# A heads stage, a merge and an out stage put into one block, with two staging tiles for keys and five for values

## The reference

```
h = rmsnorm(x) * (1 + sc1) + sh1
pq, pkv, pkr, hq, hf_f, hf_b, hi, hg, ga, gb = split(h @ w_in)
q  = (rmsnorm(pq) @ w_uq)                      # 8 heads, 64 + 32 columns each
kv = rmsnorm(pkv) @ w_ukv                      # keys and values of 8 heads, 64 + 64 columns each
o_mla = softmax(q k / sqrt(96)) v              # k also has 32 shared columns with a rotary position
o_hg  = gated linear recurrence (hq, hf, hi, hg)
mix = sigmoid(ga) * (o_mla @ w_mla_o) + sigmoid(gb) * (o_hg @ w_hg_o)
x = x + gt1 * (mix @ w_out)
x = x + gt2 * conv_glu(rmsnorm(x) * (1 + sc2) + sh2)
y = rmsnorm(x) * g_final
```

## Time and profile before

| | |
|---|---|
| median of 3 runs | 2144.15 us (2143.12 to 2145.16) |
| the profiled execution, its own time | 2142.61 us |
| its span, first to last instruction | 2140.8 us |
| PE busy | 2072.6 us, 97% of the span |
| mean granted clock of TensorE | 0.988 |
| DVE, ACT, POOL busy | 44%, 30%, 36% |
| transfers | 185.01 MB, mean 86 GB/s |

### The profile page before, as it was taken

How to read it: one execution, slowest core, us unless ns; L and a number is a source line. 1 busy time by engine, 2 the same in 40 slices (tenths; PEclk the granted TensorE clock), 3 DMA queues, 4 the chain that set the end, 5 groups by cost and what they waited for, 6 DMA issues and landing times. The chain is left out here.

```text
span 2140.8 us, 28026 instructions
## 1 busy us (share of the span) xinstructions
PE 2072.6 (97%) x11524; PEld 1927.2 (90%) x11524; DVE 948.8 (44%) x1386; ACT 649.6 (30%) x949; POOL 769.9 (36%) x512
## 2 busy tenths in 40 slices
PE   5999999999999989999989899999999999999998
PEld 4889999999999968888789778999999999999996
DVE  5326252525143047566545185245244333533466
ACT  4322323232223254766723211311111121112122
POOL 1143434444132234455526422432332232233290
PEclk9999999999999999999999999999999999999999
DMA  8753111112212284323375332211111111112132
GB/s 288 238 150 33 55 33 55 31 57 60 67 50 58 87 224 132 89 72 96 99 159 193 119 118 72 67 40 50 40 44 46 30 52 48 40 40 79 50 102 96
DMA packets 192961, 185.01 MB, mean 86 GB/s; under 512 B 55193, under 2 KB 159346, under 8 KB 192834
## 3 DMA queue, kind: packets, MB, share of 16 engines
q1 hardware_dynamic: 191538, 178.49, 28.3%
q0 software_dynamic: 1296, 4.72, 0.6%
HBM read 142.41 MB, written 40.78 MB: 86 GB/s over the span
## 5 line engine op out<-in xcount | busy, mean ns | idle before, releaser
L129 POOL TENSOR_TENSOR s_w_lo<-s_w_raw,s_w_hi 128x1024 fp32r<-128x1024 f32 x85 | 219.8, 2586 | 512.0 <-ACT s_w_hi L124 512.0
L2606 PE MATMUL s_ps<-h_hi,s_w_hi 128*128 128x384 f32 x1056 | 353.1, 334 | 0.7 <-ACT gate_pad L2438 0.7
L2606 PE MATMUL s_ps<-h_hi,s_w_lo 128*128 128x384 f32 x1056 | 352.9, 334 | 0.0
L2606 PE MATMUL s_ps<-h_lo,s_w_hi 128*128 128x384 f32 x1056 | 352.8, 334 | 0.0
L662 PE MATMUL s_psum<-h_hi,s_w_hi 128*128 128x384 f32 x984 | 332.9, 344 | 7.4 <-DVE h_lo L1330 7.4
L662 PE MATMUL s_psum<-h_lo,s_w_hi 128*128 128x384 f32 x984 | 325.7, 336 | 0.0
L662 PE MATMUL s_psum<-h_hi,s_w_lo 128*128 128x384 f32 x984 | 325.3, 336 | 0.0
L2606 PEld LDWEIGHTS s_ps<-h_hi,s_w_hi 128*128 128x128 f32 x1056 | 198.2, 188 | 1.5 <-issue 1.0
L662 PEld LDWEIGHTS s_psum<-h_hi,s_w_hi 128*128 128x128 f32 x984 | 185.5, 189 | 15.1 <-issue 12.1
L2606 PEld LDWEIGHTS s_ps<-h_lo,s_w_hi 128*128 128x128 f32 x1056 | 198.2, 188 | 0.4
L2606 PEld LDWEIGHTS s_ps<-h_hi,s_w_lo 128*128 128x128 f32 x1056 | 198.2, 188 | 0.0
(11 more groups left out here) (371 smaller groups left out, 3809.2 us busy)
## 6 DMA issues: line engine op xcount, KB each, us to landing
s_w_raw<-in_w_ffn_in SPq DMA_DIRECT2D x44, 512.0 KB, 3.9
s_w_raw<-in_w_in SPq DMA_DIRECT2D x41, 512.0 KB, 4.1
s_w_mod<-in_w_mod SPq DMA_DIRECT2D x8, 2048.0 KB, 8.1
w_raw<-in_w_ffn_out SPq DMA_DIRECT2D x11, 1024.0 KB
scratch_gates<-sig SPq DMA_DIRECT2D x48, 192.0 KB, 1.9
merge_gates<-scratch_gates SPq DMA_DIRECT2D x16, 576.0 KB, 4.3
scratch_o_mla<-o_raw SPq DMA_DIRECT2D x8, 576.0 KB, 5.0
scratch_x<-x SPq DMA_DIRECT2D x9, 512.0 KB, 2.6
```

The lines of the kernel that those rows point to most:

```text
L129: pool.tensor_tensor(flat[0], flat[1], flat[2], ALU.subtract).then_inc(self.lo_ready, 1)
L2606: mm = pe.matmul(ps[bank][:, 0:CH], a[s][:, k, :], b[:, k, j * CH:(j + 1) * CH], start=n == 0, stop=n == 3 * KD - 1)
```

## The change

The three stages after the projection share one block, one set of semaphores and one PSUM tensor. Each stage function now returns its five instruction lists, and every engine does its three lists one after the other, without a meeting in between. Where a later stage depends on an earlier one, it waits on that stage's semaphores. The merge's loads of weight chunks 2 and 3 are put in front of the loads that depend on the last head. The out stage's PSUM banks are numbered so that its first five are not those of the merge's last chunk. Slice 4 of w_out gets its tiles at a place that is free earlier. Its loads for slices 4 and 5 are issued at the end of the merge's list on SP.

In the expansion, key blocks alternate between two pairs of staging tiles, and the values use a ring of five pairs. The second key pair lies where the raw query weights `uq_raw` are, so block 1 waits until those have been read (`uq_lo_ready`). The two added value pairs lie where the second head's query tiles will be, so the split of that query waits for their stores.

The diff without the changes of indentation, cut to its core:

```diff
+V_RING = 5
-def stage_attention(nc, io, cst, lower, more, low, up, home):
-    with ExitStack() as ctx:
-        sems = Signals(nc, ctx, "s4")
+def stage_attention(nc, io, cst, sems, psum, lower, more, low, up, home):
+    sems.prefix = "s4"
...
-        uq_raw = b_only("uq_raw", [P, 3, HEADS * QH])
-        kst_hi, kst_lo = b_only("kst_hi", [P, NK], F32R), b_only("kst_lo", [P, NK], F32R)
+    raw_home = Arena(nc, b_only.at + 2 * NK * 4)
+    uq_raw = raw_home("uq_raw", [P, 3, HEADS * QH])
+    kst_hi, kst_lo = [b_only("kst_hi0", [P, NK], F32R)], [b_only("kst_lo0", [P, NK], F32R)]
+    kst_hi.append(b_only("kst_hi1", [P, NK], F32R))
+    kst_lo.append(b_only("kst_lo1", [P, NK], F32R))
+    spare_hi, spare_lo = Arena(nc, q_at + NT * 4), Arena(nc, q_at + 3 * NT * 4)
+    vst_hi += [spare_hi(f"vst_hi{i}", [P, 512], F32R) for i in range(3, V_RING)]
+    vst_lo += [spare_lo(f"vst_lo{i}", [P, 512], F32R) for i in range(3, V_RING)]
+    ps_s = [psum[:, 2 * i:2 * i + 2, :] for i in range(2)]
+    ps_m = [psum[:, 4 + i, :] for i in range(2)]
+    ps_o = psum[:, 6:8, :]
...
 # SP, heads stage: the stores name tile x % 2 (keys) and x % V_RING (values)
-        sp.wait_ge(k_stored, 32 * (h // 2 + 1))
+        sp.wait_ge(k_stored[h // 2 % 2], 32 * (h // 4 + 1))
-    sp.wait_ge(den_stored, 16 * (HEADS - 1))
-    for i in range(2):
-        sp.wait_ge(o_stored[i], 16 * HEADS // 2)
-    sp.wait_ge(g_loaded, 32)
...
 # ACT, a unit of the expansion (DVE waits for the same)
         if kind == "k":
-            if x > 0 and u == 0:
-                act.wait_ge(k_stored, 32 * x)
-            act.activation(kst_hi[:, a:z], ring(n)[:, 0:z - a], ACT.Copy).then_inc(u_act, 1)
+            if x == 1 and u == 0:
+                act.wait_ge(uq_lo_ready, 2)
+            if x >= 2 and u == 0:
+                act.wait_ge(k_stored[x % 2], 32 * (x // 2))
+            act.activation(kst_hi[x % 2][:, a:z], ring(n)[:, 0:z - a], ACT.Copy).then_inc(u_act, 1)
         if kind == "v":
-            if x >= 3:
-                act.wait_ge(v_stored[x % 3], 32 * (x // 3))
+            if x >= V_RING:
+                act.wait_ge(v_stored[x % V_RING], 32 * (x // V_RING))
...
 # ACT item H and POOL item G, head 1
+        if h == 1:
+            for i in range(3, V_RING):
+                act.wait_ge(v_stored[i], 32 * v_uses[i])
...
 # SP, merge: load_w(2) and load_w(3) first
+    else:
+        sp.wait_ge(att["w_lo"], c - 1)
+    load_w(2)
+    load_w(3)
+    for i in range(2):
+        sp.wait_ge(att["o_stored"][i], 16 * HEADS // 2)
+    sp.wait_ge(att["den_stored"], 16 * (HEADS - 1))
+    sp.wait_ge(att["x_lo"], KB)
     sp.dma_start(home.den9[:, :], ...)
-    load_w(2)
     load_x(KB)
     load_x(KB + 1)
-    load_w(3)
...
 # PE, merge
+    pe.wait_ge(att["x_lo"], KB)
     for c in range(CHUNKS_M):
         if c >= 2:
             pe.wait_ge(w_lo_ready, c - 1)
+        else:
+            pe.wait_ge(att["w_lo"], c + 1)
+        if c == 1:
+            pe.wait_ge(att["o_read"], 2 * HEADS)
 # DVE, merge, at the start
+    dve.wait_ge(att["gates"], 32)
     dve.wait_ge(last_loaded, 16)
...
 # out stage: banks, and tiles of slice 4
+    wo_hi, wo_lo = home.wo_hi + [first("wo_hi4", [P, D], F32R)], home.wo_lo + [first("wo_lo4", [P, D], F32R)]
+    first = Arena(nc, after_h + 2 * NT * 4)
-        ps = [ctx.enter_context(nc.psum_tensor(f"s8_ps{i}", [P, 512], F32)) for i in range(8)]
+    ps = [psum[:, i, :] for i in (0, 1, 2, 3, 7, 4, 5, 6)]
 # SP, out stage
+    sp.wait_ge(merge["quotient"], KD // 2)
     load_wo(4)
     load_wo(5)
+    sp.wait_ge(merge["bank"], 6 * KD)
+    sp.wait_ge(merge["gated"], 6 * KD)
+    sp.wait_ge(merge["m_lo"], KD)
 # ACT, out stage
-    for k in range(WO_HERE, KD):
+    act.wait_ge(merge["m_lo"], KD - 1)
+    wo_split(WO_HERE)
+    act.wait_ge(merge["gated"], 6 * KD)
+    for k in range(WO_HERE + 1, KD):
         wo_split(k)
 # POOL, out stage
+    pool.wait_ge(merge["m_lo"], KD)
 # PE, out stage
+    pe.wait_ge(merge["wo_lo"], WO_HERE)
     for k in range(KD):
         if k >= WO_HERE:
             pe.wait_ge(wo_lo_ready, k - WO_HERE + 1)
+        pe.wait_ge(merge["m_lo"], k + 1)
         for o in range(6):
+            if k == 0 and o in (0, 5):
+                pe.wait_ge(merge["gated"], 6 * KD - 3 + o // 5)
...
 # program
+    with ExitStack() as ctx:
+        sems = Signals(nc, ctx, "s4")
+        psum = ctx.enter_context(nc.psum_tensor("late_psum", [P, 8, 512], F32))
+        (att_sync, att_tensor, ...), att_links = stage_attention(...)
+        (merge_sync, merge_tensor, ...), merge_links = stage_merge(..., att_links)
+        out_sync, out_tensor, ... = stage_out_ffn(..., merge_links)
+        with nc.Block() as block:
+            @block.sync
+            def _(sp):
+                att_sync(sp)
+                merge_sync(sp)
+                out_sync(sp)
+            # tensor, scalar, vector and gpsimd alike
```

More of the change, by code:

```diff
@@ L2862, in program @@
     home = MergeHome(nc, base + half, upper, low.end)
-    stage_attention(nc, io, cst, lower, more, low, up, home)
-    assert lower.at <= upper and more.at <= HIGH
     mix = Arena(nc, base)
@@ L2868, in program, with _ @@
     partial = Arena(nc, base + half // 2)("merge_partial", [P, KD, NT])
-    stage_merge(nc, io, cst, home, m_hi, m_lo, partial)
     again = Arena(nc, base)
     h2_hi, h2_lo = again("h2_hi", [P, KD, NT], F32R), again("h2_lo", [P, KD, NT], F32R)
-    stage_out_ffn(nc, io, cst, base, m_hi, m_lo, h2_hi, h2_lo, home)
+    with ExitStack() as ctx:
+        sems = Signals(nc, ctx, "s4")
+        psum = ctx.enter_context(nc.psum_tensor("late_psum", [P, 8, 512], F32))
+        (att_sync, att_tensor, att_scalar, att_vector, att_gpsimd), att_links = stage_attention(nc, io, cst, sems, psum, lower, more, low, up, home)
+        assert lower.at <= upper and more.at <= HIGH
+        (merge_sync, merge_tensor, merge_scalar, merge_vector, merge_gpsimd), merge_links = stage_merge(nc, io, cst, sems, psum, home, m_hi, m_lo, partial, att_links)
+        out_sync, out_tensor, out_scalar, out_vector, out_gpsimd = stage_out_ffn(nc, io, cst, sems, psum, base, m_hi, m_lo, h2_hi, h2_lo, home, merge_links)
+        with nc.Block() as block:
[4 more added lines that the diff above has]
+                out_sync(sp)
+            @block.tensor
+            def _(pe):
+                att_tensor(pe)
+                merge_tensor(pe)
+                out_tensor(pe)
+            @block.scalar
+            def _(act):
+                att_scalar(act)
+                merge_scalar(act)
+                out_scalar(act)
+            @block.vector
+            def _(dve):
+                att_vector(dve)
+                merge_vector(dve)
+                out_vector(dve)
+            @block.gpsimd
+            def _(pool):
+                att_gpsimd(pool)
+                merge_gpsimd(pool)
+                out_gpsimd(pool)
 def constants():
```

2249 lines of the change are left out of this document (1121 added, 1128 removed).

## The result

The changed kernel takes **2132.39 us** (median of 5 runs, 2130.59 to 2133.57) against 2143.99 us, a ratio of 0.9948 with a 95% interval of 0.9936 to 0.9959. That is 11.6 us faster, where 21.0 had been forecast: the direction was right, the time lies 1.9 us above the range. The profiled execution took 2130.59 us, its span 2128.8 us, 12.0 less than before.

A forecast was written before the change was run, and what follows sets the result against it. PE sets the time, so only its idle time and slow clock afterwards can be won: 7.2 (expansion) + 4.7 (heads to merge) + 9.1 (merge to out) = 21.0 us, from 2144.15 to 2123.2 us, range 2118.5 to 2130.5.

The forecast's parts named there:

- The key tiles: Expansion: key block 2 no longer waits for key block 1's store; PE's 5.74 us wait and slow clock go, gain 6.3.
- rival C: Expansion: the wait moves from key stores to q head 2's store; gain only 17 to 19 us, 2125 to 2127; chance 0.2.
- like stretch: Expansion: PE's 14.86 us of work priced by the same work around key block 3, 8.55 us; gain 6.3.
- q_hi wait: Expansion: PE's 0.86 us wait for q_hi goes because five value tiles remove ACT's earlier store waits; gain 0.9, bounds 0 and 0.9.
- the chain of values runs ahead by two tiles: Expansion: argument given against q head 2's store, wanted again for head 4, blocking DVE; no size given.
- The value tiles: Expansion: five value tiles alone gain 0 beyond the 0.86 us q_hi wait, since PE was not waiting for them.
- Heads to merge: Border before the merge: 5.40 us pause and 2.2 slow start go, less a new 2.9 us wait; net gain 4.7.
- The new wait: Merge: PE wants weight chunk 6 at 1120.4, it comes at 1123.3; 2.9 us counted in full.
- a pause of 2.36 us: Merge: it left the clock at 1.00, so the new 2.9 us wait was given no clock loss; bound 2.2 us.
- the early weights: Merge: weight chunks 2 and 3 go out early, taking 0.51 MB or 2.4 us out of the stream that follows.
- Merge to out: Border before the out stage: 6.80 us pause and 2.3 us slow start go; gain 9.1, lower bound 8.5.
- the clear at the end: End of kernel: one clear covers all names, at most some 0.7 us, against two removed within the borders; 0 added.

The follow-up runs named there:

- late_loads: Changed kernel with the loads of head 1's k and q and head 0's v moved behind key block 2 on SP: 2128.50 us, ratio 0.9931.
- both_orders: Changed kernel with the expansion's loads moved behind key block 2 and merge weights 5 and 6 ahead of o_den and o_rows loads: 2125.67 us, ratio 0.9918.
- merge_order: Changed kernel with merge weights 5 and 6 ahead of four o_den and o_rows loads on SP, two w_out slices two chunks later: 2129.59 us.
- keys_no_values: Changed kernel with three value tiles instead of five, two key tiles kept: 2134.33 us, ratio 0.9950 to the kernel before.
- weights_back: Changed kernel with merge weight chunks 2 and 3 loaded among the x loads again, as before the change: 2134.69 us, ratio 0.9958.
- staging_only: Kernel before, three blocks kept, with only the new staging of two key tiles and five value tiles: 2143.47 us, ratio 0.9999.
- fewer_bytes: Changed kernel with both new SP load orders, leaving out four of eight o_den loads, so heads 4 to 7 use wrong sums: 2121.50 us, ratio 0.9899.

## Why the prediction was right and wrong

**The key tiles: the price was right, rival C took it.** I valued the second key tile at 6.3 us by the like stretch, with the q_hi wait 7.2. With the q store out of the way the expansion is 7.2 us shorter than with the old staging (86.95 to 79.78; 6.4 by the medians), so the like stretch was a sound measure. The step that failed is the weighing of C at 0.2 and leaving its cost out of the sum: 7.2 went into it, and the profile of after won 2.7. I even had the landing nearly right, 808.8 estimated and 809.3 seen, but partly by luck: the 2.8 us came from another store, and this one was issued earlier and took longer. The trace of before has this store landing at 809.6, 6.8 us after its issue (DMA view of 802.7 to 803, the row below), and that could have been read. It hardly moved, which was C's condition. C cost its 2 to 4 us or somewhat more: 3.1 by the medians of late_loads and after, 3.6 by those of both_orders and merge_order, and 4.8 by the profiles (the four with the new staging and the old order average 84.66, the three with late loads and ACT's list unchanged 79.87). The argument against it, that "the chain of values runs ahead by two tiles", was about the wrong thing: the store was late through its place on SP, behind loads that wait; the qf load alone held SP from 797.13 to 799.64, until the store of q head 1 had landed.

```profile
scratch_q<-qst SPq DMA_DIRECT2D x1, 432.0 KB, 6.8
```

The Trainium skill (DMA: Bandwidth & Descriptors, Specifications) gives 512 bytes as the smallest transfer for line rate. The trace agrees, as far as two stretches with different transfers can show it: between 782 and 792, with 5434 of 5669 packets under that size, the full engines moved 250 GB/s, and between 807 and 811, with 66 of 395, 412 GB/s.

**The value tiles: 0, as forecast**; the q_hi wait went. Whether its 0.9 us was won cannot be told: the expansion of keys_no_values, 85.23, lies among the four with five value tiles, 83.50 to 85.50.

**Heads to merge: 1.5 instead of 4.7.** The pause and the slow start at the border went, as forecast. The new wait was foreseen at the right place and by the right mechanism, but too small, in two terms. The weights waited 4.06 us instead of 2.9: I followed chunk 6 alone, while chunk 5 was late first, issued at 1100.25 behind four o_den and o_rows loads that had to wait for block 0 to be split. And the clock fell, which I had excluded by likeness to a pause of 2.36 us: 56.20 - 49.92 - 4.06 = 2.2 us, the very amount given as a bound; by the row behind the pause, 3.70 us at 0.54, about 1.7 of it is the clock. The Trainium skill (TensorE: Matmul & The Clock Gate, Part 1) says that an idle TensorE falls back to 1.2 GHz; the trace agrees, with 0.54 after this pause. The 2.4 us of the early weights is a term that no run confirms (weights_back).

**Merge to out: 7.9 instead of 9.1.** The pause went whole, and the start is warm. The missing 1.2 us was lost 60 us later. In the out stage PE waits 2.35 to 2.41 us for DVE in all 14 profiles. Before, the clock stayed at 1.00 there; after, it fell to 0.57. In two of the experiments with one block it did not fall, and there the part takes 160.58 and 160.57 us, 9.2 less than before: the forecast to 0.1. I had taken that stretch as unchanged.

**The sum.** Of the 9.0 us that are missing in the span, 4.5 are rival C and what it hides, 3.2 the merge's stream and its clock loss, 1.2 the clock in the out stage and 0.5 the clear at the end, which I had put at 0 with 0.7 as a bound; 0.4 came back where the expansion begins. The range ended at 2130.5, 7.4 us short of the full gain: 4 for C, 2.4 for the merge and 1 more. By the medians 9.4 are missing. What the range left out are the merge's slow clock, which I had bounded at 2.2 but not added, the out stage's 1.2 and the clear.

## What to carry to other kernels

Here a freed staging tile only moved the chain on to the next resource behind the same queue. In a like case, follow the next store of every other tile through the list of the issuing engine, loads that wait included, before counting the gain. Where a stage is bound by its transfers, an earlier start of the products is worth what the stream can follow; first look at which loads stand ahead of those that are wanted first, then at the bytes. Price a new pause of PE with its slow clock as well, and look for later pauses that the slow clock may newly hit.

## What was not expected of the hardware

The length of a pause does not by itself tell whether the clock falls. The same 2.35 to 2.41 us wait in the out stage was passed at a granted clock of 1.00 before, in staging_only, in fewer_bytes and in weights_back; in the other ten kernels the clock fell to between 0.50 and 0.68 in the stretch behind it. The stretch around it in weights_back:

```profile
1249.90:1252.30 2.40, 0.05 (x1) 0.08 (x2) 2.37 (x7) 0.00 (x0) 0.00 (x0) 1.00 0.35 108
1252.30:1254.80 2.50, 1.94 (x12) 1.55 (x13) 2.47 (x7) 1.06 (x1) 0.25 (x1) 1.00 0.48 190
```

Likewise the expansion's pause was followed by 0.66 in after (1.50 us) and by 1.00 in late_loads (1.67 us). Against the 160.57 of weights_back, the last part of the kernels with one block where it fell took 0.9 to 2.3 us longer (161.47 to 162.91). What decides between the two was not settled. Also, where the expansion begins, 752.92 to 755.26 us into the span, differs between profiles of kernels that are the same up to there, which is why single profiles were compared by parts and not by their ends.
